# Seven quadrant products for the second MLP product of a two-layer diffusion trunk, on one Trainium2 core

## What is computed

```python
def trunk(x, cond):
    for i in range(2):
        sh1, sc1, g1, sh2, sc2, g2 = split(silu(cond) @ ada_w[i] + ada_b[i], 6)
        h = rms_norm(x, norm_mix[i]) * (1 + sc1) + sh1
        x = x + g1 * (even_mixer(h) if i == 0 else pool_mixer(h))
        h = rms_norm(x, norm_mlp[i]) * (1 + sc2) + sh2
        x = x + g2 * (square(relu(h @ mlp_w1[i])) @ mlp_w2[i])   # 1024 -> 4096 -> 1024
    return rms_norm(x, final_norm)
```

## Time and profile before

| | |
|---|---|
| median of 3 runs | 2646.09 us (2644.82 to 2648.17) |
| profiled execution, its own time | 2645.16 us |
| its span, first to last instruction | 2643.4 us |
| mean granted TensorE clock | 0.988 |
| PE busy | 97% of the span, 14604 matmuls |
| DVE busy | 51% |
| ACT busy | 22% |
| POOL busy | 21% |

### The profile page before, as it was taken

How to read it: one execution, slowest core, us unless ns; L and a number is a source line. 1 busy time by engine, 2 the same in 40 slices (tenths; PEclk the granted TensorE clock), 3 DMA queues, 4 the chain that set the end, 5 groups by cost and what they waited for, 6 DMA issues and landing times.

```text
span 2643.4 us, 37530 instructions
## 1 busy us (share of the span) xinstructions
PE 2561.9 (97%) x14604; PEld 2240.7 (85%) x14604; DVE 1351.4 (51%) x2366; ACT 593.9 (22%) x982; POOL 544.8 (21%) x230
## 2 busy tenths in 40 slices
PE   7899999979999999999999999999999999999998
PEld 3878899977888888888888888888888888888887
DVE  6635752264385556554556555564444444444445
ACT  3311122142231111111111112751112111121112
POOL 6124321162121212111112111011121211212110
PEclk9999999989999999999999999899999999999999
DMA  7314523274212211211211211011010100101102
GB/s 236 149 67 142 166 96 112 95 265 168 72 33 80 71 56 56 95 56 56 71 56 56 95 56 32 25 32 33 32 48 32 48 32 32 48 32 48 32 32 80
DMA packets 126263, 199.48 MB, mean 75 GB/s; under 512 B 4420, under 2 KB 102504, under 8 KB 125800
## 3 DMA queue, kind: packets, MB, share of 16 engines
q1 hardware_dynamic: 123216, 188.76, 21.1%
q10 hardware_dynamic: 2968, 9.63, 1.2%
HBM read 167.44 MB, written 26.74 MB: 73 GB/s over the span
## 4 chain that ended last, share of the span: by engine, by line
PE 88%; DVE 5%; issue 2%; DMA 2%; ACT 2%; POOL 1%; ACTq 0%; SPq 0%; DVEq 0%; POOLq 0%
PE bank L314 83%; PE bank L1404 1%; PE bank L1432 1%; PE bank L1557 1%; DMA ada_st_in<-in_ada_w_dram 1%; PE bank L1469 1%; DVE ada_acc_in L1053 0%; PE bank L1735 0%; DVE vtok L1107 0%; DMA SB<-state_spill 0%; DVE xgm L1220 0%; POOL ringL L854 0%; DVE h1L L1227 0%; DVE X L1061 0%; ACT pF L736 0%
## 5 line engine op out<-in xcount | busy, mean ns | idle before, releaser
L854 POOL TENSOR_TENSOR ringL<-stage,ringH 128x2048 fp32r<-128x2048 f32 x82 | 392.8, 4790 | 1823.1 <-ACT ringH L532 1823.1
L1061 DVE SCALAR_TENSOR_TENSOR X<-bank,mod,X 128x512 f32<-128x512 f32 (+1 forms) x792 | 515.1, 660 | 363.4 <-PE bank L314 359.1
L314 PE MATMUL bank<-midH,ringH 128*128 128x512 f32 (+1 forms) x1536 | 546.7, 356 | 3.3 <-DVE X L1061 3.3
L314 PE MATMUL bank<-midL,ringH 128*128 128x512 f32 (+1 forms) x1536 | 544.9, 355 | 0.0
L314 PE MATMUL bank<-midH,ringL 128*128 128x512 f32 (+1 forms) x1536 | 544.7, 355 | 0.0
L314 PE MATMUL bank<-hH,ringH 128*128 128x512 f32 (+1 forms) x1248 | 447.2, 358 | 0.2 <-DVE hL L1227 0.2
L314 PE MATMUL bank<-hH,ringL 128*128 128x512 f32 (+1 forms) x1248 | 442.5, 355 | 0.0
L314 PE MATMUL bank<-hL,ringH 128*128 128x512 f32 (+1 forms) x1248 | 442.4, 355 | 0.0
L1336 DVE TENSOR_TENSOR relu<-relu 128x512 f32<-128x512 f32 (+1 forms) x192 | 146.3, 763 | 568.9 <-ACT relu L774 568.8
L774 ACT ACTIVATE relu<-bank 128x512 f32<-128x512 f32 (+1 forms) x192 | 100.9, 527 | 1375.9 <-PE bank L314 1375.9
L314 PEld LDWEIGHTS bank<-midH,ringH 128*128 128x128 f32 x1536 | 291.5, 190 | 46.1 <-DVE X L1061 6.5
(11 more groups left out here) (191 smaller groups left out, 2888.1 us busy)
## 6 DMA issues: line engine op xcount, KB each, us to landing
stage<-in_mlp_w_dram SPq DMA_DIRECT2D x64, 1024.0 KB, 5.3
ada_st_mlp<-in_ada_w_dram SPq DMA_DIRECT2D x18, 1536.0 KB, 8.3
stage<-in_ev_w_in_dram SPq DMA_DIRECT2D x14, 1024.0 KB, 5.1
ada_st_in<-in_ada_w_dram SPq DMA_DIRECT2D x8, 1536.0 KB, 9.5
ada<-in_ada_w_dram SPq DMA_DIRECT2D x8, 1024.0 KB, 13.3
x_spill<-X SPq DMA_DIRECT2D x1, 5120.0 KB, 18.5
gate_spill<-gate_st ACTq DMA_DIRECT2D x8, 640.0 KB, 3.7
gt<-gate_spill SPq DMA_DIRECT2D x20, 256.0 KB, 3.3
```

Of the source, the lines that this page charges most:

```text
L314: mm = nc.tensor.matmul(out, a, b, start=first and n == 0, stop=last and n == 2)
L854: nc.gpsimd.tensor_tensor(ringL[slot][:, :], stage[:, :], ringH[slot][:, :].bitcast(F32), ALU.subtract).then_inc(w_lo, 1)
L1061: V.scalar_tensor_tensor(out=X[:, d, cols(t)], in0=src[:, 0:TB[t][1]], scalar=gate_ap, in1=X[:, d, cols(t)], op0=ALU.mult, op1=ALU.add).th ...
```

## The change

In chunks 1 to 14 of both layers the second product for the sample tokens is regrouped. For the sample tokens it is a product of a 2 x 2 grid of weight quadrants (2 halves of the 8 output tiles by the 2 hidden tiles) with a 2 x 2 grid of hidden quadrants B (2 hidden tiles by 2 blocks of 512 tokens). Before, this is eight quadrant products for each of 4 output tiles. The change forms seven, by four weight sums S1 to S4 and four hidden sums T1 to T4 (the scheme of Strassen in Winograd's form). Some of the seven are added in PSUM onto a bank that already holds another product and has already been read once; the result reaches X through 28 additions instead of 16. The prompt tokens keep their product.

```diff
+FACTORS = {1: ("A11", "B11"), 2: ("A12", "B21"), 3: ("S4", "B22"), 4: ("A22", "T4"), 5: ("S1", "T1"), 6: ("S2", "T2"),
+           7: ("S3", "T3")}
+GOES_TO = {1: (0, 0), 2: (0, 0), 6: (0, 1), 5: (1, 1), 7: (1, 1), 3: (0, 1), 4: (1, 0)}
+CHAIN = {6: 1, 7: 6, 4: 7, 3: 5}
+FAST_SEQ = ([(1, d) for d in range(HD)] + [(2, d) for d in range(HD)]
+            + [(p, d) for d0 in range(0, HD, 2) for p in (6, 5, 7, 3, 4) for d in (d0, d0 + 1)] + [("prompt", d) for d in range(DT)])
+FAST_BANK = [(2, 3, 6, 1, 4, 5, 2, 3)[d] if p == "prompt" else (6, 1)[d % 2] if p in (2, 3, 5) else 2 + d for p, d in FAST_SEQ]
+FIRST_BANK = (0, 1, 0, 0, 0, 1)
+LO_ORDER = ["B11", "B21", "T1", "T2", "T3", "B22", "T4", "p0", "p1"]
...
+            def second_product(n):
+                p, d = FAST_SEQ[n]
+                w_name, m_name = FACTORS[p]
+                own = earlier(FAST_BANK, n)
+                pe.wait_ge(m2_ev[l], p0 + own + 1)
+                pe.wait_ge(mid_lo[l], h0 + LO_ORDER.index(m_name) + 1)
...
+            first_product(0)
+            pe.wait_ge(m2_ev[l], p0 - 4)
+            first_product(1)
+            pe.wait_ge(relu_ok[l], n0 + 1)
+            first_product(2)
+            pe.wait_ge(w_lo, UA + 2)
+            for n in range(HD):
+                second_product(n)
+            pe.wait_ge(relu_ok[l], n0 + 3)
+            first_product(3)
+            for n in range(HD, 2 * HD):
+                second_product(n)
+            pe.wait_ge(relu_ok[l], n0 + 4)
+            first_product(4)
+            pe.wait_ge(m2_ev[l], p0 + 2 * HD)
+            first_product(5)
+            pe.wait_ge(s_lo[l], ch)
+            pe.wait_ge(relu_ok[l], n0 + 6)
+            for n in range(2 * HD, 7 * HD):
+                second_product(n)
+            pe.wait_ge(mid_lo[l], h0 + FAST_MID)
+            for n in range(7 * HD, FAST_GRP):
+                prompt_product(n)
...
+            square(2)
+            V.tensor_tensor(t1, b12, b11, ALU.subtract).then_inc(t_full[l], 1)
+            for n in range(HD + 1):
+                evict(n)
+            dve.wait_ge(sqr_ok[l], n0 + 4)
+            V.tensor_tensor(t2, b22, t1, ALU.subtract).then_inc(t_full[l], 1)
+            for n in range(HD + 1, 2 * HD):
+                evict(n)
+            V.tensor_tensor(t3, b22, b12, ALU.subtract).then_inc(t_full[l], 1)
+            V.tensor_tensor(t4, b21, t2, ALU.subtract).then_inc(t_full[l], 1)
+            lower("T1")
+            lower("T2")
+            lower("T3")
+            lower("B22")
+            lower("T4")
+            lower("p0")
+            evict(2 * HD)
+            lower("p1")
+            for n in range(2 * HD + 1, FAST_GRP):
+                evict(n)
```

```diff
-        for d in range(2):
-            sp.dma_start(new_state[0, 0, d].rearrange("h d e -> d h e"), S[d][NT % 2][:, :, :]).then_inc(new_out, 16)
...
         state_loads(0)
+        for d in range(2):
+            sp.dma_start(new_state[0, 0, d].rearrange("h d e -> d h e"), S[d][NT % 2][:, :, :]).then_inc(new_out, 16)
+        sp.wait_ge(new_out, 32)
         state_loads(1)
```

More of the change, by code:

```diff
@@ L112, in advances_before @@
     return sum(1 for a in ADVANCE if a < s)
+END_NEED = [products(1, NCH - 1) + DT * (1 + (0 if n >= NS else 1 + n // 4)) for n in END_TILES]
 def after(eng, sem, n):
@@ L221, in build @@
     ones = small("ones", [P, P])
-    r_b = [at(f"relu{i}", A_V + 2 * i, [P, 512]) for i in range(3)]
+    r_b = [at(f"relu{i}", A_AD + 3 + 2 * i, [P, 512]) for i in range(3)]
     acc = at("acc", A_E + 15, [P, T])
@@ L305, in cols, with pair_pass @@
         return slice(t0, t0 + w)
-    def pair_pass(out, w_hi_ap, w_lo_ap, m_hi_ap, m_lo_ap, first, last, weights_moving=False):
+    def pair_pass(out, w_hi_ap, w_lo_ap, m_hi_ap, m_lo_ap, first, last, weights_moving=False, chained=False):
         if weights_moving:
@@ L313, in pair_pass @@
         for n, (a, b) in enumerate(terms):
-            mm = nc.tensor.matmul(out, a, b, start=first and n == 0, stop=last and n == 2)
+            mm = nc.tensor.matmul(out, a, b, start=first and n == 0, stop=last and n == 2, skip_group_check=chained)
         return mm
@@ L348, in h_part, with hidden, weight @@
         return (hH, hL)[part][:, d, cols(tb)]
+    MID_PART = {"B11": (0, 0), "B21": (1, 0), "T1": (0, 1), "B22": (1, 1), "T2": (0, 0), "T3": (1, 0), "p0": (0, 2), "p1": (1, 2)}
+    def hidden(name):
+        if name == "T4":
+            return ts4H[:, :], ts4L[:, :], r_b[0][:, :]
+        k, tb = MID_PART[name]
+        return tuple(m[:, k, cols(tb)] for m in (midH, midL, midF))
+    def weight(l, name, d):
+        if name[0] == "S":
+            i = int(name[1]) - 1
+            return tuple(m[:, i, d * P:(d + 1) * P] for m in (sumH, sumL))
+        k, n0 = int(name[2]) - 1, HD * (int(name[1]) - 1)
+        return tuple(r[(U_MLP[l] + 1) % 2][:, k * D + (n0 + d) * P:k * D + (n0 + d + 1) * P] for r in (ringH, ringL))
     def slot_free(U):
@@ L764, in hidden_hi @@
                 if g == 0:
-                    after(act, m2_mm[l], GRP * ch)
+                    after(act, m2_mm[l], products(l, ch))
                 tb = blocks[g // HT]
@@ L795, in mlp, with mlp_fast, relu, square @@
                 split_hi(U + 2, (m1_mm[l], NTB * HT * (ch + 1)), U_MLP[l] % 2)
+        def mlp_fast(l, ch):
+            U, n0, h0 = U_MLP[l] + 2 * ch, PAIRS * ch, halves(l, ch)
+            def relu(g, dst):
+                act.wait_ge(m1_mm[l], n0 + g + 1)
+                if g == 0:
+                    act.wait_ge(mid_lo[l], h0)
+                nc.scalar.activation(dst, bank[FIRST_BANK[g]][:, 0:TB[g // HT][1]], ACT.Relu).then_inc(relu_ok[l], 1)
+            def square(g, buf):
+                act.wait_ge(relu_ok[l], n0 + g + 1)
+                nc.scalar.activation(buf, buf, ACT.Square).then_inc(sqr_ok[l], 1)
+            def high(name, src=None):
+                hi, _, full = hidden(name)
+                nc.scalar.activation(hi, full if src is None else src, ACT.Copy).then_inc(mid_hi[l], 1)
+            split_hi(U + 1, (m2_mm[l], products(l, ch)), (U_MLP[l] + 1) % 2)
+            act.wait_ge(s_add[l], 4 * ch)
+            nc.scalar.activation(sumH[:, :, :], sumF[:, :, :], ACT.Copy).then_inc(s_hi[l], 1)
+            relu(0, r_b[0][:, :])
+            act.wait_ge(sqr_ok[l], n0 + 1)
+            high("B11", r_b[0][:, :])
+            relu(1, r_b[1][:, :])
+            act.wait_ge(sqr_ok[l], n0 + 2)
+            high("B21", r_b[1][:, :])
+            relu(2, r_b[2][:, :])
+            act.wait_ge(t_full[l], 4 * ch - 3)
+            high("T1")
+            relu(3, hidden("B22")[2])
+            square(3, hidden("B22")[2])
+            act.wait_ge(t_full[l], 4 * ch - 2)
+            high("T2")
+            act.wait_ge(t_full[l], 4 * ch - 1)
+            high("T3")
+            act.wait_ge(sqr_ok[l], n0 + 4)
+            high("B22")
+            act.wait_ge(t_full[l], 4 * ch)
+            high("T4")
+            relu(4, hidden("p0")[2])
+            square(4, hidden("p0")[2])
+            act.wait_ge(sqr_ok[l], n0 + 5)
+            high("p0")
+            relu(5, hidden("p1")[2])
+            square(5, hidden("p1")[2])
+            act.wait_ge(sqr_ok[l], n0 + 6)
+            high("p1")
+            split_hi(U + 2, (m1_mm[l], n0 + PAIRS), U_MLP[l] % 2)
         mlp(0, 0, first=True)
         with act.Fori(1, NCH - 1) as ch:
-            mlp(0, ch)
+            mlp_fast(0, ch)
         mlp(0, NCH - 1, last=True)
@@ L938, in mlp @@
             split_lo(U_MLP[l] + 2 * ch + 1, (U_MLP[l] + 1) % 2)
+            if l == 0 and last:
+                band_tables()
             if not (l == 1 and last):
                 split_lo(U_MLP[l] + 2 * ch + 2, U_MLP[l] % 2)
-        mlp(0, 0, first=True)
[L942 to L950, removed]
@@ L1658, in mlp @@
                     g = HT * nth + f
-                    after(pe, relu_ok[l], g - 3 if first else n0 + g - 1)
+                    after(pe, relu_ok[l], g - 3 if first else n0 + (max(g - 1, 0) if last else g - 1))
+                    if last and g == 1:
+                        pe.wait_ge(m2_ev[l], products(l, ch))
                     if first and g == HT:
@@ L1677, in mlp @@
             for nth, tb in enumerate(blocks):
-                pe.wait_ge(mid_lo[l], n0 + HT * (nth + 1))
+                pe.wait_ge(mid_lo[l], halves(l, ch) + HT * (nth + 1))
                 for d in range(DT):
                     i = DT * nth + d
-                    after(pe, m2_ev[l], GRP * ch + i - 3)
+                    after(pe, m2_ev[l], products(l, ch) + i - 3)
                     for k in range(HT):
```

200 lines of the change are left out of this document (152 added, 48 removed).

## The result

| | before | after |
|---|---|---|
| median | 2646.94 us (4 runs, 2644.82 to 2648.17) | 2622.15 us (4 runs, 2621.50 to 2623.76) |
| profiled execution, span | 2645.16, 2643.4 us | 2622.70, 2621.0 us |
| granted clock | 0.988 | 0.987 |
| PE, DVE, ACT, POOL busy | 97, 51, 22, 21% | 96, 62, 29, 31% |
| matmuls | 14604 | 14268 |

The ratio is 0.9911 (95%: 0.9898 to 0.9925), 24.8 us less. I had forecast 2597 with a range from 2585 to 2620; the sign is right, the size is half, and the time lies 2 us outside the range.

The account below looks back on a forecast made before the run. PE's matmul start-to-start time bounds every chunk. From 2645.16, 28 chunks at 1.64 us (45.9) and retention (3.4) come off and 0.5 is given away: 2596.4, as a median 2597 us; range 2585 to 2620.

Parts of the forecast that it names:

- the one on the fifth and sixth first product: After these products PE's next group needs T2's low half, ready 2.3 us early, so no stall before the 20 groups.
- Product 2's break: Third and fourth groups of the second product's product 2 wait for DVE additions onto X: 1.08 us lost a chunk.
- the saving of 12 x 0.2267 = 2.72: Wide second product drops from 96 to 84 matmuls a chunk, 2.72 us each chunk, 76.2 us over 28 chunks.
- the absence of idle time inside the 20 groups: Products 3 to 7 on PE: each group needs one 0.655 us addition against 0.68 of PE, so no stall.
- DVE's pace: Rival: burst additions follow at 0.75 us instead of 0.655, a chunk loses about 0.5, 2611 us; chance 0.11.
- PE's own queue: Rival: each of 28 groups a chunk loses 0.08 to 0.1 us to waits, +70 us, 2667, slower; chance 0.04.
- The clock: Rival: after product 2's short stalls PE runs at the 1.2 GHz level, 2631 us, or 2665 if twice a chunk; chance 0.05.
- the 1640 to 1660 row: Profile row of this kernel: PE idle 2.2 us of 20, in pieces, at clock 1.00; evidence against the clock slowing.
- The tight gap between the sums' low half and T2 in layer 0: POOL's low half of the sums ends at 26.3, DVE's T2 is due at 27.5: 1.2 us, the tightest gap.
- Retention: Reading the state before writing the new states starts PE's first retention output 3.5 us earlier; 3.4 taken if the loop shifts whole.
- Band tables: 10.6 us of POOL work moves into chunk 15 of layer 0; cost taken as 0, at most some 3 us.

Follow-up runs that it names:

- the fourth experiment: Changed kernel with sixth-relu wait moved to the burst's fourth group, product 2's first two groups before the fourth first product, T2 after their additions: 2565.02 us.
- the retention's reads alone: Kernel before, with only the spilled states read into the other buffer of each pair, ahead of the new states' write: 2641.87 us, ratio 0.9984.

## Why the prediction was half right

**The step that failed** is the one on the fifth and sixth first product: "The first group behind 34.04 wants T2's low half, done at 31.75: 2.3 us to spare". I had listed the data that the group needs, not the waits that the program puts there. One of them is for ACT's relu of the product that PE has just finished, so it can't be met in time: 0.32 us from the last matmul's start to relu's, 0.38 of relu, 0.23 to PE's restart, and 0.09 in the step behind it. The term that the sum had at nothing measures 0.90 us a chunk, 25 us in all; the experiment that moves the wait gives 2596 us and 53.44 a chunk. The prediction does count ACT's steps on that tile, for DVE's low half of p1, and didn't ask whether PE waits for the first of them too.

**Product 2's break** is right in place, cause and size: 1.05 against 1.08. So is the saving of 12 x 0.2267 = 2.72, seen in full once nothing breaks it. So is the absence of idle time inside the 20 groups: behind the restart all steps are 0.2267. The additions behind the first:

```profile
2038.08 0.75 DVE L1198 SCALAR_TENSOR_TENSOR X<-bank,mod,X 128x512 f32<-128x512 f32 x1 [2.04 <-PE bank L362]
2039.08 13.12 DVE L1198 SCALAR_TENSOR_TENSOR X<-bank,mod,X 128x512 f32<-128x512 f32 x20
```

These twenty are the other 19 wide ones and the first of the prompt, which is 0.48 long. A narrower window gives the first fifteen alone:

```profile
2039.08 9.96 DVE L1198 SCALAR_TENSOR_TENSOR X<-bank,mod,X 128x512 f32<-128x512 f32 x15
```

(9.96 - 0.75) / 14 = 0.658 us for each, against 0.655 in the forecast. The last four start 0.68 apart, as DVE has caught up and follows PE's groups.

**The rivals.** DVE's pace would have shown 0.75 there, and in the fourth experiment PE is busy 600.00 of 600 us beside it. PE's own queue: groups of three follow at 0.68 without a break. The clock: both loops show 1.00 granted, in the kernel after with three breaks a chunk as well. By the rule in the Trainium skill's page "TensorE: Matmul & The Clock Gate" ("A second HAM failure mode: psum-queue depth-cycling"), breaks between matmul groups that cycle through PSUM banks let the clock go back and forth. Neither loop shows that; the 1640 to 1660 row was the better guide. None of the rivals had the time at 2622; the range was too narrow since all of them were about how fast things run, none about a wait that I had not seen.

**POOL and DVE.** The tight gap between the sums' low half and T2 in layer 0, 1.2 us in the forecast, is 1.1: POOL ends at 927.32 + 4.62 = 931.94, T2 starts at 933.04. That the sums of chunk 1 run inside chunk 0, beside adaLN parts, I had not followed: 2.0 us.

**Retention.** This term failed too, by 3.2 us. The first output comes 3.8 us earlier, predicted 3.5, but the loop doesn't shift as a whole: of the 3.4 taken, 0.2 reach the second output product in the kernel after (117.12 against 116.95), and at most 3.1 in any run. **Band tables**: nothing, as taken: the distance between the kernels is 12.0 us both at the end of layer 0's loop and behind that chunk's stall.

**The sum again**, for the profiled execution: 2645.16 - 22.7 (chunks) + 2.0 (chunk 0) - 0.2 (retention) - 2.0 (ahead of it already) - 1.0 (the clock behind the break of 2.26) + 1.1 (the end) = 2622.4; it was 2622.70. Against the forecast's 2596.4 the chunks are 23.2 us short, the retention 3.2 and chunk 0 1.5; the last three terms, together 1.9 the other way, are luck.

## What to carry to other kernels

- When a product is reordered, write down for every group each wait that the program has there, not only the data that it needs. A wait for a reader of what PE has just finished costs its whole latency each time: here 0.32 + 0.38 + 0.23 us, and 0.1 in the next step. Put it at the first instruction that overwrites the bank.
- Fewer matmuls count only when every bank is free in time. The same seven products gave 25 us with three breaks a chunk and 80 without.
- A GpSimd and a VectorE instruction that both work in SBUF should meet where VectorE idles afterwards. Moving one 4.6 us instruction cost 0.84 us in each chunk of the layer with adaLN, 11 us in all, and nothing in the other.

## What the runs showed of the hardware

- Two kinds of meeting in SBUF. A DVE square that met a POOL instruction of 2048 columns was held to POOL's end (4.20 instead of 0.69 us). DVE's adaLN instructions of 384 columns against POOL ones of 512 slowed both: 5.75 instead of 2.20 for four, and 1.47 to 1.61 instead of 1.29 each. Additions with an input in PSUM kept 0.66 a piece beside a POOL instruction (2039.65 to 2044.27 in the kernel after) as without one.
- A break costs more than its wait: the matmul behind it is recorded 0.47 to 0.51 long and the next starts 0.31 to 0.34 later instead of 0.2267, about 0.1 us. Three breaks of up to 0.93 us in every chunk left the granted clock at 1.00.
- Code that the kernels share takes different times by the clock that PE is granted behind long waits. After one and the same break of 2.26 us in layer 0's last chunk PE ran some 13 narrow matmuls at the 1.2 GHz level before, and none directly behind it in the kernel after. In the kernel after, seven steps of 0.43 instead of 0.2267 from 613.49 on are 1.4 us, and a pooling stage with 0.80 granted instead of 0.90 went with 9 us more. Among 11 executions of one kernel (the retention's reads alone) the longest, 2649.02 us, had a mean clock of 0.986, and the shortest, 2635.51, 0.992.
